# A two-layer encoder on one core: mixture-of-experts rounds reordered by load, twelve experts as pairs and twenty as fours

## What is computed

```python
g_val, g_idx = lax.top_k(softmax(t @ w_group + b_group), 1)
e_val, e_idx = lax.top_k(softmax(chosen), 2)          # two of the group's eight
e_val = e_val / sum(e_val)
for g in range(4):
    a = einsum('td,edf->tef', t, w_gate[g])           # 1024 x 256 per expert
    u = einsum('td,edf->tef', t, w_up[g])
    act = silu(a) * u * combine[:, g, :, None]
    y = y + einsum('tef,efd->td', act, w_down[g])     # 256 x 1024 per expert
```

## Time and profile before

| | |
|---|---|
| times of three executions | 798.0, 800.01, 800.07 us; median 800.01 |
| profiled execution | 796.67 us in all, span 794.9 us |
| mean granted TensorE clock | 0.987 of full speed |
| busy, TensorE / VectorE / ScalarE / GpSimd | 738.1 / 409.2 / 277.9 / 111.2 us |
| read from memory | 242.85 MB; mean rate over the span 309 GB/s |
| MoE stage of layer 0, first gate product to last combine | 164.4 to 378.3 us |
| MoE stage of layer 1, the same | 547.1 to 760.7 us |

### The profile page before, as it was taken

How to read it: one execution, slowest core, us unless ns; L and a number is a source line. 1 busy time by engine, 2 the same in 40 slices (tenths; PEclk the granted TensorE clock), 3 DMA queues, 4 the chain that set the end, 5 groups by cost and what they waited for, 6 DMA issues and landing times.

```text
span 794.9 us, 12786 instructions
## 1 busy us (share of the span) xinstructions
PE 738.1 (93%) x5121; PEld 470.4 (59%) x5121; DVE 409.2 (51%) x913; ACT 277.9 (35%) x521; POOL 111.2 (14%) x112
## 2 busy tenths in 40 slices
PE   4877789799999999989999998999999999999896
PEld 3755655465655555544788884555655555564465
DVE  6998833644343343432786868345443343434174
ACT  6351144252221222213675746425121222222163
POOL 5697320000000000000206621000000000000000
PEclk9989999999999999999999999999999999999999
DMA  8157693659999999999657789843999999999921
GB/s 274 42 142 222 172 356 127 264 206 423 420 421 420 420 421 421 421 420 397 220 206 236 215 265 327 337 196 113 421 421 420 421 421 421 421 419 421 406 95 53
DMA packets 64244, 247.33 MB, mean 311 GB/s; under 512 B 22244, under 2 KB 23832, under 8 KB 39224
## 3 DMA queue, kind: packets, MB, share of 16 engines
q1 hardware_dynamic: 62152, 243.14, 78.3%
q0 software_dynamic: 2032, 3.35, 1.9%
HBM read 242.85 MB, written 3.06 MB: 309 GB/s over the span
## 4 chain that ended last, share of the span: by engine, by line
PE 68%; DMA 10%; DVE 10%; SPq 5%; POOL 4%; issue 1%; ACT 1%; DVEq 0%
PE PS L1951 21%; PE PS L1741 14%; PE PS L1977 11%; DMA ring<-in_moe_w_down 6%; PE PS L1987 5%; PE PS L2209 4%; DMA ring<-in_moe_w_up 3%; PE PS L1906 3%; POOL s5V L680 2%; PE PS L1921 2%; PE PS L2009 2%; POOL s5W L680 2%; SPq L471 2%; SPq L455 1%; PE PS L1839 1%
## 5 line engine op out<-in xcount | busy, mean ns | idle before, releaser
L1951 PE MATMUL PS<-ring,xw 128*64 128x256 f32 x2016 | 227.7, 379 | 6.8 <-DMA ring<-in_moe_w_up 3.0
L1951 PEld LDWEIGHTS PS<-ring,xw 128*64 128x64 f32 x2016 | 149.5, 137 | 88.8 <-issue 17.5
L1977 PE MATMUL PS<-ring,actT 128*64 128x512 f32 x512 | 116.9, 598 | 2.4 <-DMA ring<-in_moe_w_down 1.3
L1442 DVE COPY actT<-PS 128x256 f32<-128x256 f32 x32 | 13.6, 424 | 159.7 <-PE PS L1960 159.7
L959 ACT ACTIVATE ohi<-PS 128x512 fp32r<-128x512 f32 x64 | 38.2, 597 | 145.8 <-PE PS L1977 145.8
L1456 DVE TENSOR_TENSOR olo<-PS,ohi 128x512 fp32r<-128x512 f32 x64 | 44.3, 692 | 83.3 <-ACT ohi L959 83.2
L652 POOL TENSOR_TENSOR rstd<-ms,mhalf 128x2 f32<-128x2 f32 x6 | 4.2, 706 | 589.8 <-DVE ms L1126 583.4
L1977 PEld LDWEIGHTS PS<-ring,actT 128*64 128x64 f32 x512 | 34.3, 136 | 67.9 <-issue 66.2
L951 ACT ACTIVATE act<-PS,wslot 128x256 f32<-128x256 f32 x32 | 15.2, 476 | 164.9 <-PE PS L1951 164.9
L1425 DVE SCALAR_TENSOR_TENSOR act<-rows,pid 128x256 f32<-128x256 f32 x128 | 61.9, 483 | 14.0 <-DMA rows<-rows_d 10.6
L1741 PE MATMUL PS<-ringr,hTh 128*128 128x512 f32 x160 | 63.2, 395 | 1.4 <-DVE hTl L1141 1.4
(11 more groups left out here) (326 smaller groups left out, 960.4 us busy)
## 6 DMA issues: line engine op xcount, KB each, us to landing
ring<-in_moe_w_down SPq DMA_DIRECT2D x64, 1024.0 KB, 20.8
ring<-in_moe_w_up SPq DMA_DIRECT2D x64, 1024.0 KB, 18.8
ring<-in_moe_w_gate SPq DMA_DIRECT2D x62, 1024.0 KB, 16.5
ring<-in_nat_w_qkv SPq DMA_DIRECT2D x6, 2048.0 KB
ring<-in_ple_w_gate SPq DMA_DIRECT2D x4, 2048.0 KB
ring<-in_s_w_out SPq DMA_DIRECT2D x2, 2048.0 KB
ring<-in_nat_w_o SPq DMA_DIRECT2D x2, 2048.0 KB
ring<-in_s_w_in SPq DMA_DIRECT2D x1, 2048.0 KB
```

The source lines that it names most:

```text
L1951: ins = mm(PS[CAP * h_:CAP * h_ + CAP, 0, FF * u:FF * u + FF], xw[:, p % 2, k, CAP * h_:CAP * h_ + CAP], wv[h_][:, FF * k:FF * k + FF], st ...
L1977: ins = mm(PS[CAP * h_:CAP * h_ + CAP, 2 + n, :], actT[:, k, CAP * h_:CAP * h_ + CAP], wd[h_][:, k, 512 * n:512 * n + 512], start=k == 0, ...
```

## The change

The first seven experts keep their place. VectorE counts the tokens of experts 7 to 31, marks the five with most, and gives those places 7 to 11; the other twenty get places 12 to 31 in their order. Places 0 to 11 run as six pairs of 64 slots as before, places 12 to 31 as five rounds of four with 32 slots each, in four column tiles of 32. So there are 11 rounds (`NR`). The table `order` (which expert stands in a place) and `first` (its window) are made by two more small products in `cols_T`. SyncE loads the expert number from `order` into a register for every weight load from place 7 on. An expert with more than 64 (a light one with more than 32) sets the flag; the loop for it takes places of its own from `crowded`. `cols_T` moves from behind gather slice 5 to behind slice 6. The order of the rounds is written anew on TensorE, VectorE and ScalarE: gate_up(p), combine(p-1), act_transposes(p), down(p); the two projections stand ahead of the last down.

```diff
+WIDE = 12
+NR = WIDE // 2 + (NE - WIDE) // 4
+FIXED = 7
+HEAVY = WIDE - FIXED
+OFF_LIST = 4096.0
+
+
+def round_of(at):
+
+    return at // 2 if at < WIDE else WIDE // 2 + (at - WIDE) // 4
+
+
+def tiles_of(r):
+
+    if r < WIDE // 2:
+        return [(2 * r + h_, CAP * h_, CAP) for h_ in range(2)]
+    return [(WIDE + 4 * (r - WIDE // 2) + h_, CAP // 2 * h_, CAP // 2) for h_ in range(4)]
...
+            def weight(i, e, w):
+
+                if e < FIXED:
+                    return items[moe_item[i] + e][1][w][1]
+                ex = sp.value_load(order[0:1, e:e + 1], min_val=0, max_val=NE - 1)
+                return views[i][w][:, bass.ds(ex, 1), :].rearrange("p e n -> p (e n)")
...
                 if e >= 6:
-                    sp.wait_ge(S("d_done"), 2 * (NP * i + (e - 6) // 2) + 2)
-                sp.dma_start(ring[s][:, 4096:6144], down_[1]).then_inc(down_loaded[s // 2], 16)
+                    sp.wait_ge(S("d_done"), 2 * (NR * i + round_of(e - 6)) + 2)
+                sp.dma_start(ring[s][:, 4096:6144], weight(i, e, 2)).then_inc(down_loaded[s // 2], 16)
...
+                sp.wait_ge(S("first_ready"), 2 * i + 2)
                 for p in range(3, NP + 1):
                     if p < NP:
-                        sp.wait_ge(S("gate_done"), NP * i + p - 2)
+                        sp.wait_ge(S("gate_done"), NR * i + round_of(2 * p - 6) + 1)
                         for e in (2 * p, 2 * p + 1):
                             if e != EARLY:
                                 load_gate(i, e)
-                        sp.wait_ge(S("gu_done"), NP * i + p - 2)
+                        sp.wait_ge(S("gu_done"), NR * i + round_of(2 * p - 6) + 1)
                         load_up(i, 2 * p)
                         load_up(i, 2 * p + 1)
                     else:
...
+            def windows(i, r):
+
+                if r == EARLY // 2:
+                    ac.wait_ge(S("first_ready"), 2 * i + 2)
+                if r >= 2:
+                    ac.wait_ge(S("gu_done"), NR * i + r - 1)
+                for e, c0, ct in tiles_of(r):
+                    f = ac.value_load(first[0:1, e:e + 1], min_val=0, max_val=2 * T - ct)
+                    ac.activation(xw[:, r % 2, :, c0:c0 + ct], xg[:, :, bass.ds(f, ct)], ACT.Copy)\
                         .then_inc(S("xw_ready"), 1)
 
...
-                link(ve.tensor_copy(begin[:, :], PS[:, 0, TT * NE:(TT + 1) * NE]))
-                ts(first[:, :], begin[0:1, :], float(2 * T - CAP), None, ALU.min).then_inc(S("first_ready"), 1)
-                link(tt(ptmp[:, :, :, :], eq[:, :, :, :], bc(bc(begin[:, :], 1, TT), 1, 2), ALU.mult))
+                link(ve.tensor_copy(begin[:, 0:NE], PS[:, 0, TT * NE:(TT + 1) * NE]))
+                ts(first[:, 0:FIXED], begin[0:1, 0:FIXED], float(2 * T - CAP), None, ALU.min).then_inc(S("first_ready"), 1)
+                later, rest = slice(FIXED, NE), slice(0, NE - FIXED)
+                c_, k_, hv, cu, a_, b_ = [t[:, rest] for t in (count, key, heavy, cum, ta_, tb_)]
+                link(tt(c_, begin[:, FIXED + 1:NE + 1], begin[:, later], ALU.subtract))
+                link(stt(k_, c_, 64.0, iota_e[:, later], ALU.mult, ALU.add))
+                link(ve.max(top8[:, :], k_))
+                link(ts(hv, k_, top8[:, HEAVY - 1:HEAVY], None, ALU.is_ge))
+                link(ve.tensor_tensor_scan(cu, hv, ones[:, rest], 0.0, ALU.add, ALU.mult))
+                link(stt(b_, cu, 2.0, iota_e[:, later], ALU.mult, ALU.subtract))
+                link(tt(a_, iota_e[:, later], cu, ALU.subtract))
+                link(stt(b_, b_, float(2 * FIXED - 1 - WIDE), hv, ALU.add, ALU.mult))
+                link(stt(place_of[:, later], a_, float(WIDE - FIXED), b_, ALU.add, ALU.add))
+                link(ts(light[:, :], place_of[:, :], float(WIDE), CAP / 2, ALU.is_ge, ALU.mult))
+                link(stt(start_of[:, :], light[:, :], float(2 * T - CAP), begin[:, 0:NE], ALU.add, ALU.min))
+                link(stt(scr[:, :], place_of[:, :], pid[:, 0:1], iota_e[:, :], ALU.is_equal, ALU.mult, accum_out=where[:, 0:1]))
+                link(stt(scr[:, :], place_of[:, :], pid[:, 0:1], start_of[:, :], ALU.is_equal, ALU.mult, accum_out=where[:, 1:2]))
+                link(ts(shift_of[:, :], place_of[:, :], float(WIDE), CAP / 2, ALU.min, ALU.mult))
+                link(stt(shift_of[:, :], place_of[:, :], CAP / 2, shift_of[:, :], ALU.mult, ALU.add))
+                link(tt(shift_of[:, :], shift_of[:, :], start_of[:, :], ALU.subtract))
+                link(tt(limit_of[:, :], begin[:, 0:NE], light[:, :], ALU.subtract))
+                link(tt(ptmp[:, :, :, :], eq[:, :, :, :], bc(bc(shift_of[:, :], 1, TT), 1, 2), ALU.mult))
                 link(ve.tensor_reduce(bch[:, :, :], ptmp[:, :, :, :], AX.X, ALU.add))
-                link(tt(pch[:, :, :], cslot[:, :, :], bch[:, :, :], ALU.subtract))
-
-
-                link(ts(shift[:, :, :], bch[:, :, :], -float(2 * T - CAP), 0.0, ALU.add, ALU.max))
-                link(tt(shift[:, :, :], shift[:, :, :], pch[:, :, :], ALU.add))
-                link(stt(v2[:, :, :], eid[:, :, :], float(CAP), shift[:, :, :], ALU.mult, ALU.add))
-                for r in range(1, T // CAP):
-                    dst = pr1[:, :, :] if r == 1 else val[:, :, :]
-                    link(ts(dst, pch[:, :, :], float(r * CAP), float((NE - 1) * CAP), ALU.is_ge, ALU.mult))
-                    if r < T // CAP - 1:
-                        link(tt(v2[:, :, :], v2[:, :, :], dst, ALU.add))
-                    else:
-                        link(tt(slot, v2[:, :, :], dst, ALU.add))
+                link(tt(ptmp[:, :, :, :], eq[:, :, :, :], bc(bc(limit_of[:, :], 1, TT), 1, 2), ALU.mult))
+                link(ve.tensor_reduce(pch[:, :, :], ptmp[:, :, :, :], AX.X, ALU.add))
+                link(tt(pch[:, :, :], cslot[:, :, :], pch[:, :, :], ALU.subtract))
+                link(ts(pr1[:, :, :], pch[:, :, :], float(CAP), OFF_LIST, ALU.is_ge, ALU.mult))
+                link(tt(bch[:, :, :], bch[:, :, :], cslot[:, :, :], ALU.add))
+                link(tt(slot, bch[:, :, :], pr1[:, :, :], ALU.add))
                 link(ve.tensor_reduce(past[:, :], pr1[:, :, :], AX.XY, ALU.add))
+
+            def crowded(i):
+
+                link(stt(ovid[:, :, :], eid[:, :, :], float(CAP), pch[:, :, :], ALU.mult, ALU.add))
+                for r in range(1, T // CAP + 1):
+                    below = r == T // CAP
+                    link(ts(shift[:, :, :], pch[:, :, :], float(CAP if below else (r + 1) * CAP),
+                            float(-CAP * NE * 2 * T if below else (NE - 1) * CAP), ALU.is_lt if below else ALU.is_ge, ALU.mult))
+                    link(tt(ovid[:, :, :], ovid[:, :, :], shift[:, :, :], ALU.add))
...
+                ve.tensor_copy(order[:, :], PS[0:1, 4, NE:2 * NE])
+                ve.tensor_copy(first[:, FIXED:NE], PS[0:1, 4, 2 * NE + FIXED:3 * NE]).then_inc(S("first_ready"), 1)
...
+                link(ve.memset(begin[:, NE:NE + 1], float(2 * T)))
+                link(ve.tensor_copy(place_of[:, 0:FIXED], iota_e[:, 0:FIXED]))
                 route(i)
                 token_weights(i)
                 cols_evict(i)
                 ts(many[:, :], PS[0:1, 4, 0:1], 1.0, None, ALU.min).then_inc(S("many_ready"), 1)
+                crowded(i)
                 ve.wait_ge(S("rows_loaded"), 32 * (i + 1))
                 slot_weights(i, 0)
-                for p in range(NP):
-                    if p:
-                        actT_evict(i, p - 1)
+                for p in range(NR):
                     gate(i, p)
-                    if p + 1 < NP:
+                    actT_evict(i, p)
+                    if p + 1 < NR:
                         slot_weights(i, p + 1)
-                    if p:
-                        out_lo(i, p - 1)
                     select(i, p)
+                    out_lo(i, p)
                     if p == 2:
                         flag = overflow_flag(ve, i)
...
+                for c in range(2):
+                    mm(PS[0:1, 4, NE * (c + 1):NE * (c + 2)], where[:, c:c + 1], ident[:, 0:NE], start=True, stop=True)
                 pe.transpose(PS[0:10, 7, 0:P], cols[:, :], ident[:, :]).then_inc(S("cols_T"), 1)
...
+            def gate_up(i, r, u):
+
+                n = NR * i + r
+                tl = tiles_of(r)
+                wv = [ring[items[moe_item[i] + e][0]][:, 2048 * u:2048 * u + 2048] for e, _, _ in tl]
+                for e, _, _ in tl[::2]:
+                    half_arrived(pe, moe_item[i] + e, up_loaded if u else gate_loaded)
                 if u == 0:
-                    if 2 * p == EARLY:
...
+                    for w, (_, c0, ct) in zip(wv, tl):
+                        ins = mm(PS[c0:c0 + ct, 0, FF * u:FF * u + FF], xw[:, r % 2, k, c0:c0 + ct], w[:, FF * k:FF * k + FF],
                                  start=k == 0, stop=k == KD - 1)
...
-                    if k == 5:
+                    if k == 6:
                         cols_T(i)
-                gate_up(i, 0, 0)
```

(33 more changed lines are left out.)

149 lines of the change are left out of this document (69 added, 80 removed).

## The result

The changed kernel takes 813.73 us (median; 813.15 to 813.78) against 799.62 for the kernel before on the same chip: ratio 1.0178, interval [1.0161, 1.0196]. The profiled execution has a span of 812.0 us for 794.9 (+17.1). The forecast was 807.2, 7.2 us more than the 800.0 it started from; measured are 14.1. The sign is right, and the forecast size is half of what came.

A forecast was written before the change was run, and what follows sets the result against it. Memory, streaming expert weights at 420 GB/s, was taken to bound both MoE stages. Per layer, +6.2 us at the stream's start and -2.6 in the tail gave +3.6; two layers, +7.2 on 800.01, gave 807.2 us, range 801 to 817.

The forecast's parts named there:

- The bound: Both MoE stages: the weight stream from memory at 420 GB/s sets the end of the stage, not TensorE.
- D: Landing of the last down weights in a stage; fewer rounds gain 0 on it, the late stream makes it 6.2 us later.
- Fours overlap: Rounds of four on TensorE: four column tiles of 32 run side by side, costing about what a pair costs.
- Rival 5: Rounds of four: the four column tiles do not overlap, 7.5 us lost per layer, 822 us; chance 0.02.
- Routing chain: VectorE steps before the columns are ready: 4.1 us later, making the first gate product 2.4 us later.
- The start of the stream: Weight loads of experts 8 and 9 wait for round 1's later gate product: stream 6.2 us behind per layer.
- Does it fall further?: Stream after its late start: no further loss, rounds take 13.57 us, under 14.98, and later waits are met with stock.
- The tail: From the last down weights' landing to the dense product: 2.6 us shorter per layer, with two projections ahead of the last down.
- Rival 1: Clock in the tail: the low level doubles down and combine, +4 us per layer, 815 us; chance 0.09.
- Registers: SyncE's register loads ahead of weight loads: 0 to 0.1 us at the stream's start, otherwise covered by the queue.
- Rival 2: SyncE becomes the bound, from 2.06 us per register load on; 873 us at 2.5 us each; chance 0.06.
- Rivals 3 and 4: Weight stream: its late start costs less, 802.4 us, chance 0.13; or it runs faster as TensorE reads less, 795, chance 0.08.

The follow-up runs named there:

- e1: The changed kernel with the gate and up products of round 1 moved ahead of the transposes and down product of round 0; 813.86 us, ratio 1.0181.
- e4: The changed kernel with three filler matmuls in the waits of the last round of each layer; 809.95 us, ratio 1.0145.

## Why the prediction was half right

**The bound: right.** From 220 us on every stretch of 20 us of the stage in layer 0 runs at 419 to 422 GB/s (411 to 425 from 192 to 210), and all that was lost went through the start of the stream or stands at its end. "The gain on D is 0" holds: 98 us less TensorE work brought no time.

**Fours overlap: right.** 7.25 us per 128 matmuls against 7.13 for a pair. The Trainium skill ("TensorEngine Tiling (Array Packing)", Theoretical Speedup) gives up to fourfold for a dimension of at most 32; the rows agree for the product itself, and the page's number says nothing on a stage that waits on memory. Rival 5 is out.

**Routing chain: +4.1 forecast, +3.15 measured.** `cols_ready` came at 164.33 for 161.18. VectorE in order of time:

```profile
160.71 0.19 DVE L1440 TENSOR_TENSOR tab<-tab,tab 128x32 f32<-128x32 f32 x1
160.93 0.19 DVE L1441 TENSOR_TENSOR tab<-begin,tab 128x32 f32<-128x32 f32 x1
...
171.46 0.48 DVE L1488 SCALAR_TENSOR_TENSOR act<-rows,pid 128x256 f32<-128x256 f32 x1 [3.55 <-DMA rows<-rows_d]
```

A step on 32 columns follows at 0.22 us; I had taken 0.25 from steps that follow at 0.28 and read a column of weights too. That is half of the 0.95 us. The other half is the old chain, which I had put at 2.65 us for 12 steps: it has 13 and a wait, and takes 3.09 (157.21 to 160.30). So the first product was 1.36 us late, not 2.4. The rows came 3.06 us later, as forecast, and I had called that level with the product. With the product 1.07 us sooner than forecast it wasn't: round 0 waited 1.97 us for 1.19.

**The start of the stream: +6.2 forecast, +9.15 measured. This is the step that failed.** The forecast had the second gate product at 179.65; it was at 181.07. The first product gave 1.07 us less than forecast, the rows path 0.78 more, and down(0) took 5.15 us instead of 3.45, as its clock fell to 0.50 after the waits of 1.97 and 0.61 us. I had named this clock as a rival for the tail only, not for the start, where the same reordering had opened the same kind of wait. Then 0.76 us between product and issue, nearly all of it the register load that I had put at 0 to 0.1. First data came about 0.8 us behind the issue, as forecast, but the rate then climbed instead of standing at 420: the full rate counts from 1.67 us behind the issue, where the forecast had 0.9. The trace of before had shown that climb too (156 GB/s from 169 to 170, 377 from 170 to 171). Together -1.07 + 0.78 + 1.70 + 0.76 + 0.77 = 2.94 us, the whole miss of 2.95. The term of -1.07 is luck: without it the miss would be 4. The bounds of 5.0 and 8.3 were also drawn a little wide, as 0.8 and 1.9 us of chain on either side of 6.2 give 5.4 and 8.1; the measured 9.15 (8.9 by D) lies beyond the upper one.

**"Does it fall further?" was argued wrongly.** With one hole at the start I said each later wait is met with stock. In the changed kernel that is so (411 GB/s from 192 to 200 us, 425 from 200 to 210). But e1 shows that the next wait is met only because the first one came so late: with experts 8 and 9 issued sooner, the next wait runs dry.

**The tail: -2.6 forecast, -2.85 measured, but +1.9 and +2.9 given back** by the projections at a low clock. Rival 1 was true in kind, at less than its price of 4 per layer, and I gave it 0.09. The measured 813.73 lies above the 804 to 811 of the forecast alone, about at its upper bound (800.0 + 13.6), and inside 801 to 817, whose top had been raised for a part of this rival. The Trainium skill ("TensorE: Matmul & The Clock Gate", HAM oscillation) describes short work between waits for transfers as falling back each time. The rows agree in the main: 0.57 to 0.83 in most of the stretches of the fours, 5.37 and 6.50 us for projections of 3.65. They don't agree on each time: the first down of layer 0 kept the full clock in e4. My argument against it, that TensorE has much to do in the last 18 us, overlooked the wait of 2 to 3 us for `in_p` right before the transposes.

**Registers: 0 to 0.1 forecast, 0.7 us each at an exposed place.** Constant addresses gave back 2.5 us in all, of which 1.1 was the clock of a projection. Rival 2 does not decide, since 0.7 is far under 2.06. **Rivals 3 and 4** are out: the rate did not rise when TensorE rested.

**The level.** The sum was a difference on the profiled execution and was put on the median. The same difference is 17.1 us between the spans and 14.1 between the medians; the stages above explain the former.

What stays open: what decides whether the clock falls after a wait of about 2 us, and where the last 1.8 of the 4.3 us come from that leaving out the sorting brought in layer 1.

## What to carry to other kernels

Where a stream of transfers sets the time, ask of every reordering on the compute engines which wait at the head of the stream's issuer it moves, and check the next rounds too: one hole may be hiding another. Ask it for the clock as well, at every place where the reordering opens a wait on the path. A saving in TensorE's work that is not on the path opens waits, and what follows a wait of 2 us on the path may run at half clock; here three filler matmuls in such waits (0.9 us each at full clock) were cheaper than that. Load registers ahead of the wait, not between the wait and the transfer that everybody is waiting for.
